# Gate weights folded through the block-diagonal projections in an mLSTM decoder step on one core

## The reference, cut to what matters

```python
xm, z = jnp.split(x @ p['mlstm_w_up'][j], 2, axis=-1)
x_ext = jnp.concatenate([conv_buf.astype(xm.dtype), xm], axis=1)
xc = jax.nn.silu(causal_depthwise_conv(x_ext, p['mlstm_conv_w'][j], p['mlstm_conv_b'][j], s))
q = headwise_proj(xc, p['mlstm_w_q'][j])      # blocks of 4 x 4
k = headwise_proj(xc, p['mlstm_w_k'][j])
v = headwise_proj(xm, p['mlstm_w_v'][j])
qkv = jnp.concatenate([q, k, v], axis=-1)
ig = (qkv @ p['mlstm_w_ig'][j] + p['mlstm_b_ig'][j]).astype(jnp.float32)
lf = jax.nn.log_sigmoid((qkv @ p['mlstm_w_fg'][j] + p['mlstm_b_fg'][j]).astype(jnp.float32))
```

## Time and profile before

| | us |
|---|---|
| median of 3 runs | 1645.46 |
| lowest, highest | 1638.66, 1646.36 |
| profiled execution | 1643.55 |
| its span (first to last instruction) | 1641.8 |
| tensor engine busy in the span | 1361.0 (83%) |
| vector engine, scalar engine busy | 530.6 (32%), 197.8 (12%) |
| HBM traffic | 532.82 MB |

### The profile page before, as it was taken

The page is one execution under the profiler, slowest core; times in us unless marked ns, Lnnn a source line. Parts: engine busy times, 40 slices in busy tenths (PEclk is TensorE's granted clock), DMA queues, the critical chain, the costliest instruction groups (busy, mean ns, idle before and its releaser), DMA issues.

```text
span 1641.8 us, 18713 instructions
## 1 busy us (share of the span) xinstructions
PE 1361.0 (83%) x7690; PEld 769.6 (47%) x7690; DVE 530.6 (32%) x1223; ACT 197.8 (12%) x435; POOL 32.0 (2%) x66
## 2 busy tenths in 40 slices
PE   8998999898999856855855899999997657765867
PEld 5764334276765422322432477787644323322424
DVE  5535777644123211220220333640322202211222
ACT  2233322120020000000000021200200000000001
POOL 4001000000000000000000000000000000000000
PEclk7998999899999989888987999999999779788979
DMA  6410999994835999999999974443499999999994
GB/s 207 154 52 33 345 383 388 389 352 156 346 128 234 428 429 428 428 427 429 428 428 429 415 281 154 161 183 131 199 390 427 427 428 427 428 429 429 428 429 196
DMA packets 101341, 532.82 MB, mean 325 GB/s; under 512 B 6409, under 2 KB 24009, under 8 KB 76365
## 3 DMA queue, kind: packets, MB, share of 16 engines
q1 hardware_dynamic: 97472, 526.25, 79.1%
q10 hardware_dynamic: 3360, 5.09, 0.9%
q0 software_dynamic: 448, 0.62, 0.2%
HBM read 492.45 MB, written 39.49 MB: 324 GB/s over the span
## 4 chain that ended last, share of the span: by engine, by line
PE 59%; DMA 30%; DVE 7%; issue 2%; ACT 1%; SPq 1%; DVEq 0%
DMA arena<-in_moe_w_up 28%; PE bank L879 23%; PE bank L1239 10%; PE bank L1261 5%; PE bank L1219 3%; PE bank L1274 3%; DVE arena L1598 2%; PE bank L1001 2%; PE bank L1247 1%; PE bank L1144 1%; PE bank L1153 1%; DMA arena<-in_mlstm_w_up 1%; SPq L388 1%; PE bank L933 1%; DMA out_C_s<-arena 1%
## 5 line engine op out<-in xcount | busy, mean ns | idle before, releaser
L1239 PE MATMUL bank<-arena,hT 128*32 128x512 f32 x2048 | 266.7, 680 | 196.0 <-DMA arena<-in_moe_w_up 185.4
L879 PE MATMUL bank<-hT,arena 128*128 128x288 f32 x1024 | 257.6, 413 | 2.1 <-DMA arena<-in_mlstm_w_up 2.1
L1239 PEld LDWEIGHTS bank<-arena,hT 128*32 128x32 f32 x2048 | 76.5, 123 | 372.8 <-issue 372.3
L879 PEld LDWEIGHTS bank<-hT,arena 128*128 128x128 f32 x1024 | 196.2, 193 | 56.8 <-DMA arena<-in_mlstm_w_up 2.2
L1758 DVE TENSOR_TENSOR arena<-arena,bank 64x512 f32<-64x512 f32 x32 | 22.1, 692 | 531.6 <-ACT arena L749 531.6
L1219 PE MATMUL bank<-arena 128*128 128x128 f32 (+1 forms) x864 | 153.8, 308 | 1.2 <-DVE arena L1733 0.9
L1261 PE MATMUL bank<-arena 128*32 128x512 f32 x1024 | 127.5, 641 | 21.3 <-DVE arena L1762 20.6
L1219 PEld LDWEIGHTS bank<-arena 128*128 128x128 f32 (+1 forms) x864 | 117.3, 187 | 48.7 <-issue 14.4
L879 PE MATMUL bank<-arena 128*128 128x288 f32 x512 | 130.4, 415 | 0.0
L879 PEld LDWEIGHTS bank<-arena 128*128 128x128 f32 x512 | 97.7, 193 | 31.7 <-issue 3.5
L749 ACT ACTIVATE arena<-bank 64x512 f32<-64x512 f32 x32 | 18.8, 588 | 756.8 <-PE bank L1239 756.8
(11 more groups left out here) (345 smaller groups left out, 1040.5 us busy)
## 6 DMA issues: line engine op xcount, KB each, us to landing
arena<-in_moe_w_gate SPq DMA_DIRECT2D x64, 2048.0 KB, 29.9
arena<-in_moe_w_up SPq DMA_DIRECT2D x64, 2048.0 KB, 32.3
arena<-in_moe_w_down SPq DMA_DIRECT2D x64, 2048.0 KB, 25.0
arena<-in_state_mlstm_C SPq DMA_DIRECT2D x32, 1024.0 KB, 8.5
out_C_s<-arena SPq DMA_DIRECT2D x32, 1024.0 KB, 10.8
arena<-in_mlstm_w_up SPq DMA_DIRECT2D x8, 2048.0 KB, 11.4
arena<-in_cmlp_w_in SPq DMA_DIRECT2D x8, 2048.0 KB, 16.9
arena<-in_mlstm_w_down SPq DMA_DIRECT2D x4, 2048.0 KB, 19.3
```

The source lines that it names most:

```text
L879: ins = mm(B[m % 4][:, 0:NT], w[:, k, 128 * i:128 * i + 128], rhs(k), start=(k == 0), stop=(k == kt - 1))
L1239: ins = mm(B[j][CAP * i:CAP * i + CAP, :], xq[h][:, k, CAP * e:CAP * e + CAP], w[i][:, k, :], start=(k == 0), stop=(k == KD - 1), skip_gro ...
```

## The change

The gate sums are taken straight from `xc` and xm. Since q is xc times a block-diagonal matrix, q times the gate weights is xc times a folded weight, and the same holds for k and v. `fw` holds the folded weights: 48 tiles of 8 columns, the q and k parts added together, so that 16 remain for xc and 16 for xm. They are made by four matmuls with a 0/1 matrix (`row_of_block`) that brings row 4n + i of a block to all four rows of it (`folded_gates`, behind up tile 2), and by multiplications with the block entries on the vector engine (`fold_gates`, ahead of the convolution of tile 2).

`gate_part(m)` now has three matmuls on xc (288 columns), the prompt part of xm (256) and its sample part (32), and stands behind up tile m + 3; the last three stand in the q and k loop. v by features and its copies are gone. The gate sums, the activations and the scans now stand among the q and k steps; the first two copies of k are the scalar engine's. The transposes of the convolution rows follow the values by token, use banks 0 and 1, and are copied by the scalar engine. Keys by token stand ahead of the transposes of the gate rows, and the twelve fillers are gone.

Copies of q that were all ahead of the gates now stand between its steps. The diff, cut to its core:

```diff
--- before.py
+++ after.py
+        fw = at(arena, after + 5632, 48, 8)
+        fwt = at(arena, after + 6016, 48, 8)
+        row_of_block = at(arena, after + 6400, 4, P)
         wqkv = at(high, 10048 + 576, 4, 48)
         nraw = at(high, 11200, 512)
         cst = at(high, 11200, 2, DH)
...
+            def query_out(m):
+
                 act.wait_ge(s("qkv_mm"), m + 1)
                 if m == 0:
                     act.wait_ge(s("raw_tr"), 5)
                 act.activation(qT[:, m, :], B[m % 2][:, 0:NT], ACT.Copy).then_inc(s("q_out"), 1)
-                if m >= 2:
-                    act.wait_ge(s("gate_part"), m - 1)
-                act.activation(vtr[:, m % 2, :], B[4 + m % 2][:, 0:NT], ACT.Copy).then_inc(s("v_out"), 1)
...
+            for m in range(5):
+                if m == 2:
+                    silu(KI - 1)
+                query_out(m)
+                if m < 2:
+                    act.activation(kT[:, m, :], B[2 + m % 2][:, 0:NT], ACT.Copy).then_inc(s("q_out"), 1)
...
             ins.then_inc(s("gates_act"), 1)
+            query_out(5)
+            query_out(6)
             act.wait_ge(s("gates_pe"), 1)
...
+            act.activation(gt[0:4, 1, :], B[4][0:4, 0:NT], ACT.Identity, bias=gb[:, 0:1]).then_inc(s("gates_act"), 1)
+            act.activation(gt[0:4, 2, :], B[5][0:4, 0:NT], ACT.Identity, bias=gb[:, 1:2]).then_inc(s("gates_act"), 1)
+            query_out(7)
+            query_out(8)
 
             act.wait_ge(s("gates_dve"), 1)
             act.activation(gt[0:4, 4, :], gt[0:4, 3, :], ACT.Exp, scale=-1.0).then_inc(s("gates_act"), 1)
+            query_out(9)
             act.wait_ge(s("gates_act"), 4)
             act.wait_ge(s("consts"), 3)
             act.activation(gt[0:4, 3, :], gt[0:4, 4, :], ACT.Ln, bias=ones[0:4, 0:1]).then_inc(s("gates_act"), 1)
...
+            for m in range(10, KI):
+                query_out(m)
             for i in range(3):
                 value_out(0, i)
+            for n in range(4):
+                act.wait_ge(s("cv_tr"), n + 1)
+                act.activation(cvout[0:27, 512 * n:512 * n + 512], B[n % 2][0:27, :], ACT.Copy).then_inc(s("cv_out"), 1)
...
+            def folded_gates():
+
+                pe.wait_ge(s("raw_out"), 5)
+                for i in range(4):
+                    ins = mm(B[4 + i][:, 0:384], row_of_block[:, i, :],
+                             wif[:].rearrange("p t n -> p (t n)"), start=True, stop=True)
+                ins.then_inc(s("raw_tr"), 1)
+
+            def gate_part(m):
+
+                if m == 0:
+                    pe.wait_ge(s("raw_out"), 7)
+                pe.wait_ge(s("xm_out"), 3 * m + 3)
+                pe.wait_ge(s("xc"), 2 * m + 2)
+                mm(B[6][0:8, 0:NT], fw[:, m, :], xc[:, m, :], start=(m == 0), stop=(m == KI - 1), skip_group_check=True)
+                mm(B[6][32:40, 0:NPROMPT], fw[:, 32 + m, :], xe[:, m, 3:XS], start=(m == 0), stop=(m == KI - 1),
+                   skip_group_check=True)
+                mm(B[6][64:72, NPROMPT:NT], fw[:, 32 + m, :], xms[:, m, :], start=(m == 0), stop=(m == KI - 1),
+                   skip_group_check=True).then_inc(s("gate_part"), 1)
+
+            def behind_up(m):
+
+                if m == 0:
+                    small_weights()
+                elif m == 2:
+                    folded_gates()
+                elif m > 2:
+                    gate_part(m - 3)
+
             dense("up", 4, 4, 512, KD, lambda k: hT[:, k, :], "xm_mm", lambda m: pe.wait_ge(s("xm_out"), 3 * m + 3),
-                  first=normed(0), after=lambda m: small_weights() if m == 0 else None)
...
+                  first=normed(0), after=behind_up)
...
+                if m < 2:
+                    pe.wait_ge(s("xm_out"), 3 * (KI - 3 + m))
+                else:
+                    pe.wait_ge(s("q_out"), m - 1 + min(m - 2, 2))
                 mm(B[m % 2][:, 0:NT], bd[:, 0, m, :], xc[:, m, :], start=True, stop=True)
...
+                if m < 2:
+                    pe.wait_ge(s("xm_out"), 3 * (KI - 1 + m))
+                elif m < 4:
+                    pe.wait_ge(s("q_out"), 2 * m - 2)
+                else:
+                    pe.wait_ge(s("k_out"), m - 3)
+                mm(B[2 + m % 2][:, 0:NT], bd[:, 1, m, :], xc[:, m, :], start=True, stop=True).then_inc(s("qkv_mm"), 1)
+                if 1 <= m < 4:
+                    gate_part(KI - 4 + m)
+                elif m == 5:
+                    pe.wait_ge(s("gates_act"), 1)
+                    pe.wait_ge(s("masks"), 1)
+                    mm(B[4][0:4, 0:NT], gfold[0:96, 0:4], gt[0:96, 0, :], start=True, stop=True)
+                    mm(B[5][0:4, 0:NT], gfold[0:96, 4:8], gt[0:96, 0, :], start=True, stop=True).then_inc(s("gates_pe"), 1)
...
-            pe.wait_ge(s("cv_out"), 4)
+            pe.wait_ge(s("gates_act"), 3)
+            pe.wait_ge(s("k_out"), KI - 2)
             for i in range(3):
                 values_by_token(0, i)
+            pe.wait_ge(s("q_out"), KI + 2)
+            pe.wait_ge(s("cv27"), 2)
+            for m in range(KI):
+                if m in (8, 12):
+                    pe.wait_ge(s("cv_out"), m // 4 - 1)
+                ins = tr(B[(m // 4) % 2][0:27, 128 * (m % 4):128 * (m % 4) + 128], cv27[:, m, :], ident[:])
+                if m % 4 == 3:
+                    ins.then_inc(s("cv_tr"), 1)
             scores(0)
             pe.wait_ge(s("vtok"), 3)
-            keep_busy(3, 12)
+            for i in range(3):
+                keys_by_token(0, i)
+            pe.wait_ge(s("cv_out"), 4)
             pe.wait_ge(s("gates_dve"), 2)
             for j, (t0, n) in enumerate(TOK):
                 tr(B[2][0:n, 128 * j:128 * j + 128], rows[:, t0:t0 + n], ident[:])
             tr(B[3][0:NB, 0:H], catA[0:4, NT:NT + 8], ident[0:4, 0:4]).then_inc(s("gates_pe"), 1)
-            for i in range(3):
-                keys_by_token(0, i)
...
+            dve.wait_ge(s("consts"), 2)
+            for i in range(4):
+                copy(row_of_block[:, i, :].rearrange("p (n d) -> p n d", d=4),
+                     ident[:, i:P:4].unsqueeze(2).to_broadcast([P, 32, 4]))
...
+            def fold_gates():
+
+                dve.wait_ge(s("raw_tr"), 6)
+                r = [B[4 + i][:, 0:384].rearrange("p (t n) -> p t n", n=8) for i in range(4)]
+                w = [wqkv[:, i, :].unsqueeze(2).to_broadcast([P, 48, 8]) for i in range(4)]
+                link(tt(fw, r[0], w[0], ALU.mult))
+                for i in range(1, 4):
+                    link(tt(fwt, r[i], w[i], ALU.mult))
+                    link(tt(fw, fw, fwt, ALU.add))
+                tt(fw[:, 0:16, :], fw[:, 0:16, :], fw[:, 16:32, :], ALU.add).then_inc(s("raw_out"), 1)
...
             W = XE - 3
             for m in range(KI):
+                if m == 2:
+                    fold_gates()
                 dve.wait_ge(s("xm_out"), 3 * m + 3)
                 if m >= 2:
...
                 ins.then_inc(s("conv"), 1)
-            for m in range(KI):
+            def key_out(m):
+
                 dve.wait_ge(s("qkv_mm"), m + 1)
                 copy(kT[:, m, :], B[2 + m % 2][:, 0:NT]).then_inc(s("k_out"), 1)
 
+            for m in range(2, 4):
+                key_out(m)
             dve.wait_ge(s("xc"), 2 * KI)
             copy(cv27[:, :, 0:3], xe[:, :, NPROMPT:NPROMPT + 3]).then_inc(s("cv27"), 1)
             copy(cv27[:, :, 3:27].rearrange("p m (b c) -> p m b c", c=3), sample_view_all(xe, 4)).then_inc(s("cv27"), 1)
-            for n in range(4):
-                dve.wait_ge(s("cv_tr"), n + 1)
-                copy(cvout[0:27, 512 * n:512 * n + 512], B[4 + n % 2][0:27, :]).then_inc(s("cv_out"), 1)
+            for m in range(4, 7):
+                key_out(m)
 
             gi, gf, tmp, lf, ones4, fs, a, ap = (gt[0:4, n, :] for n in (1, 2, 3, 4, 5, 6, 7, 8))
             radd = gt[0:4, 9, :]
...
             link(dve.memset(gt[0:4, 9, NPROMPT:NT:SB], -1.0e38))
+            key_out(7)
             dve.wait_ge(s("gates_act"), 3)
             link(ts(tmp, gf, -1.0, None, ALU.mult))
             tt(tmp, tmp, gf, ALU.max).then_inc(s("gates_dve"), 1)
+            for m in range(8, 12):
+                key_out(m)
             dve.wait_ge(s("gates_act"), 5)
             link(stt(lf, gf, 0.0, tmp, ALU.min, ALU.subtract))
             link(dve.tensor_tensor_scan(fs, ones4, lf, 0.0, ALU.mult, ALU.add))
+            key_out(12)
             link(tt(a, gi, fs, ALU.subtract))
             link(copy(ap, a))
+            key_out(13)
             link(tt(gt[0:4, 8, NPROMPT:NT:SB], gt[0:4, 7, NPROMPT:NT:SB], m0[:], ALU.max))
             Am = catA[:, 0:NT]
             link(dve.tensor_tensor_scan(Am, radd, ap, NEG, ALU.add, ALU.max))
+            key_out(14)
+            key_out(15)
             bs = "p (b s) -> p b s"
```

72 lines of the change are left out of this document (16 added, 56 removed).

## The result

The changed kernel takes 1632.43 us (median of 9 runs, 1629.58 to 1634.55), the kernel before 1639.3 us beside it (9 runs, 1634.9 to 1646.36). The ratio of the means is 0.9949, 95% interval 0.9931 to 0.9967, so about 8.4 us less (5.4 to 11.3); the medians differ by 6.9 us. The profiled executions differ by 10.4 us (span 1631.4 against 1641.8). A later set of runs gave 0.9922 (0.9898 to 0.9946). The forecast was 1634, 10.5 us less.

A forecast was written before the change was run, and what follows sets the result against it. The tensor engine's instruction stream was taken as the bound: 22.9 us saved between up and first spread, less 12.4 paid in up, gives 10.5 us net. From 1643.55 that gives 1633.0; the forecast was 1634, range 1626 to 1642.

The forecast's parts named there:

- Folding and its wait: Up stage: four folding matmuls add 2.6 us, and the first gate part behind them waits 0.6 us (0 to 1.4).
- Gate parts: Up stage: thirteen gate parts behind tiles 3 to 15 at 0.71 us each add 9.2 us (7.8 to 10.5).
- The q and k loop: Behind up: pairs 15.5, three gate parts 2.1, gate sums 1.0, their wait 0.5, table-load waits 2.0; 21.1 us.
- waits at steps 11 and 12: q and k loop: tensor engine waits for q copies behind the scalar engine's Exp and Ln table loads, 0.75 and 1.25 us.
- From the loop to the spread: Last k copy, values, transposes, scores, keys, gate rows, their pieces and six fillers before the first spread matmul: 15.0 us.
- The sum: End of up to first spread 36.1 instead of 59.0 us, less 12.4 paid in up: 10.5 us saved, forecast 1634.
- B: Before the first spread: low clock falls ahead of the fillers, doubling 1.5 and 2.97 us; 4.4 us, 1638.4; chance 0.15.
- E: Low-clock stretch after the pause is gone or shorter, giving back 5 to 6 us; 1628; chance 0.07.
- C: q and k loop: each table load holds the scalar engine another 1.28 us, copies 2.6 later; 1636.6; chance 0.04.
- D: State stage: its DMA traffic fixes its end and swallows the gain; about 1644.5; chance 0.07.
- F: Gate parts with three stream lengths do not run side by side, 1.74 us more each, 27.8 us; 1662; chance 0.07.

The follow-up runs named there:

- gates_out: Changed kernel without the gate parts of tiles 1 to 12; first q matmul 94.22 us instead of 103.33; total 2094.88 us, with more expert matmuls.
- third_bank: Changed kernel with three PSUM banks in turn for q instead of two; ratio 0.9936 to the kernel before.
- ln_later: third_bank's edit on the changed kernel, plus Ln three q copies later and its vector pieces behind step 13's k copy; ratio 0.9968 to the kernel before.
- gates_after: Changed kernel with the gate chain, from gate sums on, started behind all q,k steps; ratio 0.9945 to the kernel before.
- fill_pause: Changed kernel with twelve filler matmuls added in the pause of the first state step; ratio 0.9952 to the kernel before.
- packed: Changed kernel with two tiles' gate parts issued together in four column groups, eight slots instead of sixteen; ratio 0.9927 to the kernel before.
- v_back: Changed kernel with the two v-by-features matmuls issued again in each of sixteen q,k steps, result unread; ratio 1.0004 to the kernel before.
- packed_rows: packed with its first two tiles whole, plus gate-row transposes ahead of the scores, on the changed kernel; 1624.89 us, ratio 0.9887 to the kernel before.

## Why the prediction came out right, step by step

- **Folding and its wait**: 2.6 us and 0.6 foreseen, 2.6 (39.56 to 42.14) and 0.66 measured. An operation of 384 elements on the vector engine took 0.56 us, as read between the neighbouring rows, and the next began 0.59 us behind its start (42.34 to 42.93 and on).
- **Gate parts**: 0.71 foreseen, 0.77 measured (0.76 by gates_out). I had taken the start-up behind a part as 0.11 from one row of the q, k, v loop; in up it is 0.19, which is what the row behind the down tiles had shown. Thirteen parts: 0.8 us too little, the largest miss in the sum. Up ended 0.6 later than forecast.
- **The q and k loop**: 21.1 foreseen, 22.0 from 103.33 to the end of the last k. Pairs 0.97 as said; the wait for the sums 0.40 in its row (0.5), sums 1.06 (1.0); waits at steps 11 and 12 of 0.69 and 0.93 in their rows. These rows count a wait from the end of the matmul before it; the forecast counted from start to start, and so counted 0.85 and 1.09 us were lost (117.69 to 119.03 and 119.59 to 121.17, less 0.49 each) where 0.75 and 1.25 were foreseen. The three gate parts were 0.2 dearer; the rest of the 0.9 I have not split. The place of the two waits and their cause were right, but third_bank and ln_later show that to remove them is not to gain them.
- **From the loop to the spread**: 15.0 foreseen, 14.4 measured (k copy 0.68, values 2.9, transposes 2.2, scores 3.1, keys 1.3, gate rows 0.6, pieces 2.4, fillers 1.25). One of the six fillers is not recorded, so some 0.2 of the pieces' 2.4 is the fillers', and both are then as foreseen (2.2 and 1.5). The gate rows were ready 8 us before use (127.5 to 135.5) where the prediction had said that they would not be late, and gates_after shows that this slack was not needed.
- **The sum**: 36.4 instead of 36.1, 13.0 instead of 12.4: 9.6 us at the first spread, 10.4 in the span, 8.4 (5.4 to 11.3) by the ratio. Some of the fit is luck. In the 36.4 the loop's 0.9 too little and the 0.6 too much behind it cancel for the most part. And 1634 lies 1.6 us from the measured median because two more misses cancel: the saving was put at 10.5 us and came out at 8.4, and the time of the kernel before, which the forecast took between 1643.55 and 1645.46 from one profile and three runs, was 1640.5 in the mean of nine.
- **Rivals**: In this profile B and E did not come, and the half clock moved with the work (144 to 157 after, 154 to 168 before); the granted clock was 1.00 over all of 100 to 142 us, with the sixteen transposes at 128.8 to 131.1 and the pause ahead of the fillers in it. The transposes that by the Trainium skill (TensorE: Matmul & The Clock Gate, Part 4: PE-mode transpose) do not count as busy in the same way thus cost no clock in this profile. That B stayed away is luck as far as the runs show: in fill_pause, whose program is the changed kernel's up to that place, the clock fell at 138.0, 0.3 us ahead of the first spread matmul, and in packed ahead of the fillers' end. B's price was too high: from the first spread matmul to the first store the early half clock cost 1.0 us (10.4 instead of 9.4) and not 2.97, because the pause behind it shrank (1.30 us in packed, 2.97 in the changed kernel), and in packed another 1.0 in the fillers. C: Exp began at 118.15, 0.01 us behind its table load's end, and Ln 0.02 behind the other. The drain of 1.38 us that the Trainium skill (ScalarE: Activation LUTs, What ACT_TABLE_LOAD costs) gives is not in these rows; where page and row differ, the row decides. D: gates_out moved the first store by 7.6 and the down slice by 12.3 us, so what is sooner there is not lost, to within the 4 us of a profile. F: three lengths of stream run side by side (0.58 us a gate part), and by packed so do four groups.

What stays open is how the two halves of the change would stand alone: v by features can't go without the fold, so "the gates' half is worth little" rests on v_back, which keeps the early gates and adds the v matmuls, on its interval of 0.19% (3 us) to either side, and on its first store, 2.4 us ahead of the kernel before. What the half clock is worth stays open too, since no two runs differ in it alone.

## What to carry to other kernels

Where one engine's stream is the bound, count that stream, and take off the waits that it covered: the 32 matmuls removed were 16 x 0.66 = 10.6 us of it, and put back they cost 7.4 us at the first spread matmul (9.0 by the ratio), because they also cover waits that lie bare without them. A chain that was moved "beside" other work was worth nothing, because other work had covered it. Before a wait is attacked, look what the late engine has to do next: twice here it came back one step on. And a narrow matmul in a column group is paid by the slot, so fill all four groups before adding a slot.

## What the runs showed of the hardware that I had not expected

- Six 8-column matmuls in four column groups cost 0.79 us of the stream, three in three groups 0.77; of that, 0.18 to 0.19 is not in the rows of the small matmuls but in the full-width tiles behind them (7.96 for two instead of 7.78, and 4.08 instead of 3.89).
- The length of the half-clock stretch behind the first state step went from 7 to 27 us with small edits ahead of it (6.6 fill_pause, 10 packed_rows, 13 after, 27 packed), and the ratio does not follow it (0.9952, 0.9887, 0.9949 and 0.9922, 0.9927). Its place moved as well: in gates_out, ln_later, packed and fill_pause the clock fell ahead of the first spread matmul, in the others 4 to 8 us behind it. Where it fell ahead, the first store came 10.4 us behind the first spread matmul (12.0 with the twelve fillers), elsewhere 9.2 to 9.4.
- The first-store time fixes the end of the state stage only to within some 8 us: 247.5 to 255.9 us from there to the down projection in thirteen profiles, in which TensorE's waits for loads of C went from 0 to 5.0 us in no order of the edits.
